# One weight chunk of the 30th expert in thirteen transfers of unequal shape

## The reference, cut to what matters

```
h = x + token_mixer(rmsnorm(x))            # x @ w_in, short conv, retention, @ w_out
top_vals, top_idx = top_k(hn @ w_router + b_router, 4);  gates = softmax(top_vals)
for each expert e, for the tokens that chose it:
    u   = xb @ w_up[e] + b_up[e]           # w_up[e]: 1024 x 2048, float32, 8 MB
    act = min(u_glu, 7) * sigmoid(1.702 * u_glu) * (clip(u_lin, -7, 7) + 1)
    y   = act @ w_down[e] + b_down[e]      # w_down[e]: 1024 x 1024, float32, 4 MB
h = h + sum over the 4 experts of gate * y;   out = rmsnorm(h)
```

## Time and profile before

| | |
|---|---|
| median of 3 runs | 1089.9 us (1089.86 to 1089.92) |
| profiled execution: time | 1088.76 us |
| profiled execution: span of its core | 1086.9 us |
| TensorE (PE) matmuls busy | 1064.6 us, 98% |
| VectorE (DVE), ScalarE (ACT), GpSimd (POOL) busy | 358.8, 152.7, 12.1 us |
| moved | 431.47 MB, mean 397 GB/s |

### The profile page before, as it was taken

How to read it: one execution, slowest core, us unless ns; L and a number is a source line. 1 busy time by engine, 2 the same in 40 slices (tenths; PEclk the granted TensorE clock), 3 DMA queues, 4 the chain that set the end, 5 groups by cost and what they waited for, 6 DMA issues and landing times.

```text
span 1086.9 us, 13159 instructions
## 1 busy us (share of the span) xinstructions
PE 1064.6 (98%) x5670; PEld 446.8 (41%) x5671; DVE 358.8 (33%) x569; ACT 152.7 (14%) x302; POOL 12.1 (1%) x28
## 2 busy tenths in 40 slices
PE   8999999999999999999999999999999999999997
PEld 6888764333333333333333333333333333333332
DVE  3455534322222222222222222223332222232234
ACT  2121144111111101111111111011111101001113
POOL 1000000000000000000000000000000000000002
PEclk9999999999999999999999999999999999999999
DMA  9875939999999999999999999999999999999994
GB/s 296 306 273 198 404 147 364 417 428 429 429 434 429 429 432 431 430 432 430 428 436 430 426 433 432 427 436 429 425 441 426 426 439 425 425 429 425 428 415 158
DMA packets 42923, 431.47 MB, mean 397 GB/s; under 512 B 4680, under 2 KB 20076, under 8 KB 25328
## 3 DMA queue, kind: packets, MB, share of 16 engines
q1 hardware_dynamic: 42256, 430.41, 94.6%
q10 hardware_dynamic: 608, 0.20, 0.1%
HBM read 427.00 MB, written 3.48 MB: 396 GB/s over the span
## 4 chain that ended last, share of the span: by engine, by line
PE 80%; DMA 19%; issue 0%; DVE 0%; ACT 0%; POOLq 0%; DVEq 0%; ACTq 0%; POOL 0%
PE bank L996 34%; PE bank L1015 15%; DMA ring_all<-in_w_up 14%; PE bank L675 9%; PE bank L1060 5%; DMA ring_all<-in_w_down 4%; PE bank L970 3%; PE bank L1007 2%; PE bank L788 2%; PE bank L978 2%; PE bank L988 1%; PE bank L637 1%; PE bank L1053 1%; PE bank L1072 1%; PE bank L796 1%; PE bank L1098 1%
## 5 line engine op out<-in xcount | busy, mean ns | idle before, releaser
L996 PE MATMUL bank<-ring_all,work 128*64 128x512 f32 x2048 | 484.6, 600 | 7.5 <-DMA ring_all<-in_w_up 7.4
L996 PEld LDWEIGHTS bank<-ring_all,work 128*64 128x64 f32 x2048 | 134.7, 136 | 257.2 <-issue 247.6
L1015 PE MATMUL bank<-ring_all,work 128*64 128x512 f32 x992 | 225.3, 596 | 1.4 <-DMA ring_all<-in_w_down 1.4
L1811 DVE TENSOR_TENSOR h_tok<-h_tok,bank 128x1024 f32<-128x1024 f32 (+1 forms) x67 | 81.7, 1220 | 236.8 <-PE bank L1060 230.9
L1015 PEld LDWEIGHTS bank<-ring_all,work 128*64 128x64 f32 x992 | 68.5, 137 | 130.5 <-issue 129.6
L675 PE MATMUL bank<-work,ring_all 128*128 128x264 f32 x384 | 86.9, 386 | 0.2 <-issue 0.2
L1781 DVE TENSOR_TENSOR work<-bank,bias_up 128x1024 f32<-128x1024 f32 x32 | 39.1, 1223 | 125.5 <-PE bank L1007 125.5
L675 PEld LDWEIGHTS bank<-work,ring_all 128*128 128x128 f32 x384 | 72.5, 190 | 12.4 <-issue 0.2
L1060 PE MATMUL bank<-work 64*128 64x512 f32 (+1 forms) x268 | 75.1, 637 | 0.0
L1798 DVE TENSOR_TENSOR work<-work 128x512 f32<-128x512 f32 x32 | 22.2, 692 | 108.6 <-ACT work L1399 108.5
L1383 ACT ACTIVATE work<-bank 128x264 f32<-128x264 f32 x32 | 12.5, 391 | 316.1 <-PE bank L988 316.1
(11 more groups left out here) (230 smaller groups left out, 544.3 us busy)
## 6 DMA issues: line engine op xcount, KB each, us to landing
ring_all<-in_w_up SPq DMA_DIRECT2D x44, 4096.0 KB, 35.0
ring_all<-in_w_down SPq DMA_DIRECT2D x22, 4096.0 KB, 35.9
ring_all<-in_w_up SPq DMA_DIRECT2D x32, 2048.0 KB, 27.4
ring_all<-in_w_down SPq DMA_DIRECT2D x15, 2048.0 KB, 39.2
ring_all<-in_w_up SPq DMA_DIRECT2D x16, 1024.0 KB, 9.7
ring_all<-in_w_in SPq DMA_DIRECT2D x13, 1024.0 KB, 5.1
ring_all<-in_w_down SPq DMA_DIRECT2D x10, 1024.0 KB, 9.8
ring_all<-in_w_out SPq DMA_DIRECT2D x4, 1024.0 KB, 10.6
```

What stands on the lines that cost most here:

```text
L996: mm = pe.matmul(bank[half * CAP:(half + 1) * CAP, up_bank(n) + b, :].rearrange("q (k p) -> q p k", k=KT), x, src[:, half * FF + b * 512:h ...
L1015: mm = pe.matmul(bank[half * CAP:(half + 1) * CAP, Y, :], av[:, 2 * i + k, :], src[:, k * D + half * 512:k * D + (half + 1) * 512], start= ...
L1811: tt(rows, rows, bank[0:m, b:b + 2, :], ALU.add).then_inc(comb_added, 1)
```

## The change

The chunk `("u", 29, 0)`, number 172, is no longer one transfer of 128 rows. SyncE asks for its rows 0 to 31 as one transfer, which still raises `landed[2]`, and then for the rows 32 to 127 as twelve transfers of eight rows (16 KB each row, 128 KB each transfer), which raise the new semaphore `uneven_in` by 16 each. Before the first step of `ups(29)` TensorE waits for `landed[2]` as before and also for `uneven_in` to reach 192. The bytes, their source and their destination are the same.

```diff
+UNEVEN = (29, 0)
+EVEN_ROWS = 32
+FEW_ROWS = 8
@@ the other semaphores
             half_used = sem("half_used")
+            uneven_in = sem("uneven_in")
@@ SyncE, for s in range(RING, LAST)
                     sp.wait_ge(mm_done, s - RING + 1)
+                    if s == place["u", UNEVEN[0], UNEVEN[1]]:
+                        sp.dma_start(ring(s)[0:EVEN_ROWS], chunk_src(stream[s])[0:EVEN_ROWS]).then_inc(landed[s % RING], 16)
+                        for p0 in range(EVEN_ROWS, P, FEW_ROWS):
+                            sp.dma_start(ring(s)[p0:p0 + FEW_ROWS], chunk_src(stream[s])[p0:p0 + FEW_ROWS]).then_inc(uneven_in, 16)
+                        continue
@@ TensorE, await_half
                     if half == halved and s - 1 not in pairs:
                         r, count = signal[s]
                         pe.wait_ge(landed[r], count)
+                    if half == 0 and s == place["u", UNEVEN[0], UNEVEN[1]]:
+                        pe.wait_ge(uneven_in, 16 * ((P - EVEN_ROWS) // FEW_ROWS))
```

## The result

| | before | after |
|---|---|---|
| median (6 runs each) | 1090.0 us (1089.9 to 1091.9) | 1106.8 us (1106.5 to 1109.8) |
| ratio, 95% interval | | 1.0156 (1.0146 to 1.0166) |
| profiled execution: time, span | 1088.76, 1086.9 us | 1109.77, 1107.8 us |

The kernel is 16.8 us slower by the medians. The profiled execution of after is the longest of its six, 3.0 us above their median, and that of before lies 1.3 us under its own; so the two traces stand 20.9 us of span apart. What follows accounts for these 20.9 us.

What follows compares the result with a forecast made beforehand. The prediction held the kernel bound by the weight stream's landing from chunk 172 on. Median 1089.9 plus 16.3 us of delay, issues and clock counted as nothing, gave 1106.2 us; own range 1097 to 1113, wider range 1092 to 1119.

Steps and rivals of the forecast that it cites:

- 16.3: Delay in us forecast for the stream at chunk 172: 21.3 for the loaded eight engines, or 16.3 with their lead of 5.
- The 3.2 of `b_down`: Slowing factor read from a 32-row transfer beside the full stream, applied to twelve rows of 0.617 us: 23.7 us.
- The bound: From chunk 172 on transfers are the slower side, 79.6 against 75.9 us; chunk 188 ties the end to the stream.
- The load: Eight-row transfers run on eight engines, which carry 14 rows of chunk 172 in place of 8: 3.7 us more.
- The narrow destination: Writing few partitions at a time, eight here, slows the divided chunk's transfers; the deciding cost, 3.2 times their share.
- Engines that don't meet share nothing: Half the engines run some 5 us behind at the divided chunk, so the lower delay, 16.3 us, was taken.
- Issues: SyncE's thirteen issues for chunk 172 take 9.9 us, covered by over 30 us of queued work; uncovered 5.3 us.
- The wait and the clock: TensorE idles about 12 us at 980; second wait free, lower clock counted 0, range 0 to 2 us.
- (a): Rival, load only at chunk 172: narrow writes free, loaded eight engines are the late group; +3.7, 1093.6 us; chance 0.07.
- (b): Rival, not slower: loaded eight lead by 5 us, late group relieved, chunk 188 lands in time; 1089.3 us; chance 0.13.
- (c): Rival, full sharing: four engines writing neighbouring rows take turns at every transfer; +27.2 less 0 to 5, 1112 to 1117; chance 0.18.
- (d): Rival: eight rows spread over all 16 engines, so only covered issues are added; 1089.9 us; chance 0.03.

Runs made afterwards that it cites:

- narrow4: Changed kernel's thirteen transfers moved to the first chunk of expert 4 (chunk 22, about 230 us), chunk 172 one transfer again: 1109.2 us, ratio 1.0173.
- farsrc29: Changed kernel with the same destinations, but each eight-row transfer reads rows twelve apart in HBM: 1105.6 us, ratio 1.0141.
- fardst29: Changed kernel with neighbouring source rows kept, but each transfer writes partitions four apart: 1102.7 us, ratio 1.0113.
- wide29: Changed kernel's thirteen transfers, same load per engine, but each takes every fourth row, so its rows lie four partitions apart: 1103.6 us, ratio 1.0118.
- four29: Changed kernel with chunk 172 as one transfer of 96 rows and four of eight neighbouring rows: 1102.8 us, ratio 1.0114.
- sixteen29: Changed kernel with chunk 172 as eight transfers of 16 neighbouring rows, even load on all engines: 1103.9 us, ratio 1.0120.
- halves29: Changed kernel with chunk 172 as two transfers of 64 rows, even load: 1102.1 us, ratio 1.0105.
- owners29: Changed kernel with chunk 172 as eight transfers of eight rows four apart, partitions 0 to 63 only, other half not loaded: 1089.4 us, ratio 0.9991.
- others29: Changed kernel with chunk 172 as eight transfers of eight rows four apart, partitions 64 to 127 only, other half not loaded: 1100.9 us, ratio 1.0096.
- cols29: Changed kernel with chunk 172 in thirteen transfers of all 128 rows and 320 columns each: 1091.5 us, ratio 1.0012.

## Why the prediction was right, and where it was not

**The number.** 1106.2 us forecast, 1106.8 measured, in the likeliest case's own range. Against the trace it is less good: the sum for the span was 1103.2 and it was 1107.8. Of the 4.6 us between, 4.3 are the distance of the two profiled executions from their medians, 3.0 above and 1.3 below.

That 16.3 and 16.8 agree so well is in part luck. The 3.2 of `b_down` counts the time that all 16 engines lost beside one small transfer, and the sum then puts it on the twelve rows of eight engines alone. Kept as it was read, it gives 2.2 x 96 x 0.617 / 16 = 8.1 us of pace for the twelve transfers, and with the load of 3.7 us about 12: too little. Measured were 16.5 us of pace, which is 264 us of engine time, 4.5 times what the 96 rows take themselves; as a factor like the prediction's that is 5.5. And the sum takes off 5 us for a lead that was no lead of all eight. A cost put on half of the engines made the number larger, a factor too low and that lead made it smaller, and they nearly cancel.

**The bound: right.** Chunk 188 tied the end to the stream, and a late stream moved it one for one: 21.4 us at chunk 172, 20.95 at chunk 188, 20.9 in the span. `narrow4` shows it for a delay made far earlier.

**The load: a part, shown only in sums.** Some profiled executions were late before the divided chunk, which has to be added. It was asked for at 937.80 us in before, at 937.42 in `farsrc29` (297 GB/s, 12.1 us of pace), 938.65 in `fardst29` (324 GB/s, 9.6 us), 938.72 in `wide29`, 937.70 in `four29`, 939.10 in `sixteen29` (291 GB/s, 12.7 us) and, 4.0 us late, in `halves29`:

```profile
941.83 0.56 SPq L549 DMA_DIRECT2D ring_all<-in_w_up  x1
```

Lost pace, load and this lateness together then fall short of what the span has grown by no more than 1.2 us in every run, from 0.1 in `narrow4` (its chunk was asked for 0.25 us early) to 1.2 in `sixteen29`. Without the load, the five runs that have its 3.7 us would fall short by 3.8 to 4.8, while the two with even load stand at 1.2 and 0.6.

**The narrow destination: the failing step.** "It isn't small rows or the source but the narrow destination (32 partitions) that I hold for the cause." The source is out and the destination in, as said. But narrow it need not be: two transfers of 64 rows lose 11.6 us, and eight rows at a time lose nothing if they are the right ones. What costs, as far as the runs show, is a partition written by another engine than the one that writes it in the stream. That fewness adds to it isn't shown: neighbouring rows cost 16.8 us against 13.2 for spread ones, but six of the twelve eight-row transfers of `wide29` are ones of `owners29`, which are free, and the other six ones of `others29`. The factor of 3.2 was too low, as said above, and in `others29` the 11.1 us of lost pace beside 64 rows make it 5.5 too. If the 32 rows of `b_down` go to engines that don't own them either, that is why it could be carried over at all; this was not tried by itself.

The Trainium skill, "SBUF — State Buffer", section "Door 1: The DMA port swizzle", would make it 29 us for the twelve transfers, by two ports at a time: an estimate from the page's figure. Measured were 16.8 us in place and 18.6 in `narrow4`, of which the load is 3.7; the page's rule overstates this kernel's price. Its section "Can I just issue two DMAs to hit both halves?" has the two halves serialize, at 6% more bandwidth than one; beside a full stream `halves29` paid 11.6 us for a chunk of 4.9.

**"Engines that don't meet share nothing": half wrong.** The 16.3 rested on the loaded eight having a lead of 5 us over the others. The trace of after speaks against two clean groups. The slow stretch has all 16 engines busy at 167 to 259 GB/s, so they do meet, and the chunk ahead, already in the queue, kept TensorE waiting for 4.53 us: presumably an engine that was behind with its older rows was slowed by one in front of it. At the tail the share falls to 0.30 and 0.12, where before it stood at 0.57 and 0.50: a few engines are last and not eight.

Two other traces say more on which engines lagged. These are the tails of `halves29` (even load) and of `owners29`, where the other eight engines carry nothing of the chunk and so have 8 x 0.617 = 4.9 us less to do:

```profile
1082.00:1084.00 2.00, 2.00 (x14) 0.74 (x12) 0.87 (x1) 0.00 (x0) 0.00 (x0) 1.00 0.57 216
1084.00:1086.00 2.00, 2.00 (x14) 0.79 (x12) 1.15 (x2) 0.00 (x0) 0.00 (x0) 1.00 0.53 205
```

```profile
1066.00:1068.00 2.00, 2.00 (x14) 0.71 (x14) 1.03 (x1) 0.00 (x0) 0.00 (x0) 1.00 0.26 101
1068.00:1070.00 2.00, 2.00 (x14) 0.71 (x16) 1.15 (x2) 0.00 (x0) 0.00 (x0) 1.00 0.18 59
```

With even load the tail of before is kept. In `owners29` 0.26 and 0.18 of 16 are four and three engines that still last to 1070 us, and the relief of the other eight didn't reach them; the rest of the late ones are gone. So, if it is the same eight engines that carry every eight-row transfer, three or four of them belonged to the late group. They had no lead in which the 3.7 us could fit, and through them the load reaches the end, as the sums have it. This is read from one execution each.

**Issues: right, too high.** Thirteen took 7.4 us and not 9.9, 0.59 for each of the twelve, and were hidden: `cols29` pays 32.8 us for its thirteen and loses 1.1 us in all.

**The wait and the clock: right that they are free, mis-sized and misplaced.** Two waits, 4.53 and 9.68, in place of one of 12 us at 980. The clock fell and 32 matmuls took 4.6 us longer than at the full one, and the stream took it back: the later waits are 0.95 and 0.85 us, so TensorE still stood waiting for the stream at chunk 188, and `narrow4` lost as much (18.6 us by its median) at full clock.

**The rivals.** (a), load only, is excluded by the rate; (b), by the same; (c), full sharing, overstates by at least 5 us; (d) by every run with few rows.

## What to carry to other kernels

Where a stream of 128-row transfers never empties its queue, divide a transfer by columns and not by rows: thirteen column pieces cost 1.1 us, any division into rows that was tried on the whole chunk 11.6 us or more, two halves among them. The column pieces kept SyncE for 32.8 us, which was free only because over 30 us of work lay in the queue. And price a delay of such a stream at its full length wherever it happens (tried at 240 and at 980 us), however much slack TensorE has there. Read the rate beside the share: these 16 engines stood at share 1.0 and moved 170 GB/s.

## What the runs showed of the hardware that was not expected

- Eight-row transfers to the lower half of the partitions left the stream at 425 GB/s; the same to the upper half took it to 308 GB/s over 40 us. They look alike in code, and why the slowing takes in all 16 engines is open.
- All 16 engines are held up, and read as busy: at 167 GB/s the share stays at 1.04. In `others29` a row took 1.23 us on the average of 20 us, twice the usual. The missing pace is in the rate alone.
- A slow chunk can delay the one asked for before it: TensorE waited 4.5 us for that one here. That the engines aren't at the same chunk is the likely reason.
- An issue of few rows has no fixed price on SyncE: 0.59 us in after, 0.34 in `narrow4` (twelve in 4.03 us), 0.76 in the four of L512.
